# The last projection of a two-block model kernel: the fourth tile of tokens runs two steps behind the other three, activations are split two steps sooner, and the last pair's transposes move among the second half's products

## The reference

```
u = h @ w_in;  q, fz, i, gate = split(u, 4)          # 1024 -> 4 * 2048
o = hgrn2_chunk_scan(q, k, v, b)                     # 16 heads of 128
o = o * rsqrt(mean(o * o) + EPS) * norm_g            # per head
y = (o * silu(gate)) @ w_out                         # 2048 -> 1024: the last projection
h = h + y;  out = rms_norm(h, final_g)
```

## Time and profile before

| | us |
|---|---|
| median of 3 runs | 1507.29 |
| lowest, highest | 1507.28, 1510.85 |
| profiled execution, its own time | 1509.23 |
| span of the profile | 1507.5 |
| TensorE's mean granted clock | 0.99 of full |
| PE busy | 1454.2 (96%) |
| DVE busy | 871.4 (58%) |
| ACT busy | 563.1 (37%) |

### The profile page before, as it was taken

One profiled execution on the slowest core, in us unless ns is written; L12 is line 12 of the kernel. 1 busy time (PEld: TensorE's weight loads), 2 busy tenths in 40 slices (PEclk: granted clock), 3 DMA queues, 4 the chain that ended last, 5 costly groups with the idle time before them and its releaser, 6 DMA issues.

```text
span 1507.5 us, 18485 instructions
## 1 busy us (share of the span) xinstructions
PE 1454.2 (96%) x7204; PEld 1208.6 (80%) x7204; DVE 871.4 (58%) x1716; ACT 563.1 (37%) x1022; POOL 0.2 (0%) x4
## 2 busy tenths in 40 slices
PE   4999998999999999899999899999999999999897
PEld 4788887888888888888888787888888888888686
DVE  7877766443333335655547435325777878778435
ACT  6423345422232223533223234334444544445231
POOL 0000000000000000000000000000000000000000
PEclk9999999999999999999999999999999999999999
DMA  8646441353323333223233232332222222222121
GB/s 326 226 152 220 173 154 47 120 197 98 93 94 95 97 97 98 72 97 126 70 108 102 70 112 84 99 98 70 71 70 71 65 63 71 70 71 71 56 70 57
DMA packets 43719, 158.31 MB, mean 105 GB/s; under 512 B 4848, under 2 KB 5232, under 8 KB 43632
## 3 DMA queue, kind: packets, MB, share of 16 engines
q1 hardware_dynamic: 43632, 157.12, 31.9%
HBM read 155.00 MB, written 2.10 MB: 104 GB/s over the span
## 4 chain that ended last, share of the span: by engine, by line
PE 89%; DVE 6%; ACT 3%; issue 1%; DMA 1%; SPq 0%; ACTq 0%; DVEq 0%
PE PS L463 27%; PE PS L465 27%; PE PS L464 27%; PE PS L738 1%; PE PS L786 1%; PE PS L749 1%; PE PS L790 1%; PE PS L780 1%; DVE WL L915 1%; PE PS L758 1%; PE PS L766 1%; DVE RAW L885 1%; PE PS L814 1%; DMA X<-in_x 1%; DVE X L1030 1%
## 5 line engine op out<-in xcount | busy, mean ns | idle before, releaser
L463 PE MATMUL PS<-HH,WH 128*128 128x512 f32 (+1 forms) x1152 | 452.1, 392 | 4.4 <-ACT TMP L1688 2.3
L465 PE MATMUL PS<-HH,WL 128*128 128x512 f32 (+1 forms) x1152 | 437.3, 380 | 0.0
L464 PE MATMUL PS<-HL,WH 128*128 128x512 f32 (+1 forms) x1152 | 436.4, 379 | 0.0
L915 DVE TENSOR_TENSOR WL<-RAW,WH 128x1024 fp32r<-128x1024 f32 x225 | 273.6, 1219 | 83.7 <-ACT WH L1589 83.4
L1589 ACT ACTIVATE WH<-RAW 128x1024 fp32r<-128x1024 f32 x225 | 236.9, 1056 | 174.9 <-PE PS L465 134.6
L463 PEld LDWEIGHTS PS<-HH,WH 128*128 128x128 f32 x1152 | 218.2, 189 | 43.1 <-issue 3.7
L465 PEld LDWEIGHTS PS<-HH,WL 128*128 128x128 f32 x1152 | 217.9, 189 | 42.0
L464 PEld LDWEIGHTS PS<-HL,WH 128*128 128x128 f32 x1152 | 218.5, 190 | 37.0 <-issue 1.0
L463 PE MATMUL PS<-WH,ZH 128*128 128x512 f32 x400 | 157.0, 392 | 3.9 <-issue 3.9
L464 PE MATMUL PS<-WL,ZH 128*128 128x512 f32 x400 | 156.8, 392 | 0.0
L465 PE MATMUL PS<-WH,ZL 128*128 128x512 f32 x400 | 156.6, 391 | 0.0
(11 more groups left out here) (244 smaller groups left out, 1647.8 us busy)
## 6 DMA issues: line engine op xcount, KB each, us to landing
RAW<-in_w_fc SPq DMA_DIRECT2D x64, 512.0 KB, 3.5
RAW<-in_hgrn_in SPq DMA_DIRECT2D x64, 512.0 KB, 3.5
RAW<-in_ada SPq DMA_DIRECT2D x43, 512.0 KB, 4.7
RAW<-in_pool_in SPq DMA_DIRECT2D x40, 512.0 KB, 3.5
RAW<-in_w_in SPq DMA_DIRECT2D x27, 512.0 KB, 4.3
RAW<-in_pool_out SPq DMA_DIRECT2D x16, 512.0 KB, 3.5
RAW<-in_hgrn_out SPq DMA_DIRECT2D x16, 512.0 KB, 3.5
RAW<-in_w_out SPq DMA_DIRECT2D x8, 512.0 KB, 4.0
```

The source lines that it names most:

```text
L463: e.matmul(out, wh, xh, start=first, stop=False)
L464: e.matmul(out, wh, xl, start=False, stop=False)
L465: return e.matmul(out, wl, xh, start=False, stop=last)
L915: e.tensor_tensor(lo, raw(i), hi.bitcast(F32), ALU.subtract).then_inc(taken.sem, taken(i))
```

## The change

It keeps every product and every instruction's work; PE has 6256 rows of instructions before and after, and only their order differs.

1. `group` for the first half is replaced by `first_half`: 10 steps instead of 8. Step s issues k = s of tiles 0 to 2 (s < 8), then k = s - 2 of tile 3 (s > 1). A weight unit is released by tile 3's odd k, so two steps later. `mixing(15)` still starts after step 1.
2. ACT and DVE split k = 0 to 5 at n = 18 to 23 of head 15 (before: k = 0 to 3 at n = 20 to 23), and k = 6, 7 at steps 0 and 1 of the first half.
3. In the second half the transposes of heads 14 and 15 stand after k = 4 and k = 6 of tiles 0 to 2 (before: after k = 0 and k = 1). DVE and ACT take the weight units that used to stand behind them first.

```diff
--- before.py
+++ after.py
@@ -795,15 +795,6 @@
                     norms.append(two_norms(h - 1))
                 yield
 
-            def open_product(first, k, tiles):
-                hi, lo = (x[:, 512 * (k % 2):512 * (k % 2) + 512] for x in place(first + k // 2))
-                for t in tiles:
-                    b, cols = out_bank("hout", t, 1), slice(128 * t, 128 * t + 128)
-                    if k == 0:
-                        claim(b)
-                    m = three(PS[b][:, :], HH[:, k, cols], HL[:, k, cols], hi, lo, k == 0, False)
-                return m
-
             def two_norms(h):
 
                 for i in range(2):
@@ -816,12 +807,37 @@
                     m.then_inc(banks.full[RBK], banks.fill(("ho norm", h + i), RBK))
                     yield
 
+            def out_product(first, k, t, n):
+
+                hi, lo = (x[:, 512 * (k % 2):512 * (k % 2) + 512] for x in place(first + k // 2))
+                b, cols = out_bank("hout", t, n), slice(128 * t, 128 * t + 128)
+                if k == 0:
+                    claim(b)
+                return three(PS[b][:, :], HH[:, k, cols], HL[:, k, cols], hi, lo, k == 0, False)
+
+            def first_half():
+
+
+                first = p.unit
+                for step in range(10):
+                    if step < 8:
+                        if step % 2 == 0:
+                            next_unit()
+                        e.wait_ge(hlo.sem, hlo.of("hout", step))
+                        for t in range(3):
+                            out_product(first, step, t, 0)
+                    if step > 1:
+                        k = step - 2
+                        m = out_product(first, k, 3, 0)
+                        if k % 2:
+                            m.then_inc(read.sem, read("w", first + k // 2))
+                            wfree[first + k // 2] = read.sem, read.n
+                    yield
+
             norms = []
             turn, side = iter(()), iter(())
             for h in range(17):
-                steps = project(h) if h < 16 else group(
-                    None, [out_bank("hout", t, 0) for t in range(4)], True, "hout")
-                for n, _ in enumerate(steps):
+                for n, _ in enumerate(project(h) if h < 16 else first_half()):
                     if n in SIDE or h == 16:
                         next(side, None)
                         next(turn, None)
@@ -833,19 +849,21 @@
 
 
             turn = norms.pop()
+            next(turn)
             first = p.unit
-            for q in range(4):
-                next_unit()
-                for kk in range(2):
-                    open_product(first, 2 * q + kk, range(3))
+            for k in range(8):
+                if k % 2 == 0:
+                    next_unit()
+                for t in range(3):
+                    out_product(first, k, t, 1)
+                if k in (4, 6):
+                    next(turn)
                     next(turn, None)
-                    next(turn, None)
-            run(turn)
-            for q in range(4):
-                for kk in range(2):
-                    m = open_product(first, 2 * q + kk, (3,))
-                m.then_inc(read.sem, read("w", first + q))
-                wfree[first + q] = read.sem, read.n
+            for k in range(8):
+                m = out_product(first, k, 3, 1)
+                if k % 2:
+                    m.then_inc(read.sem, read("w", first + k // 2))
+                    wfree[first + k // 2] = read.sem, read.n
             rows("hout", 16, 8)
 
 
@@ -1529,11 +1547,10 @@
                 for n, _ in enumerate(project(h) if h < 16 else group()):
                     if n == (0 if h == 16 else 3) and gates:
                         gates.pop()()
-                    if h == 15 and n >= 20:
-                        split_z(n - 20)
-                    if h == 16 and n < 3:
-                        for k in ((4, 5), (6,), (7,))[n]:
-                            split_z(k)
+                    if h == 15 and n >= 18:
+                        split_z(n - 18)
+                    if h == 16 and n < 2:
+                        split_z(6 + n)
                     if n == 10 and prep:
                         ready_steps = prep.pop()
                     if n >= 10 or h:
@@ -1551,18 +1568,17 @@
 
 
             turn = norms.pop()
+            next(turn)
             first = p.unit
-            for q in range(4):
-                p.unit += 1
-                lo_to(min(p.unit + 2, first + 4))
-                for kk in range(2):
-                    next(turn, None)
-                    next(turn, None)
-            run(turn)
+            p.unit += 4
+            lo_to(first + 4)
             z_first(8)
-            lo_to(first + 6)
-            for q in range(4):
-                lo_to(first + 6 + q)
+            next(turn)
+            next(turn)
+            lo_to(first + 5)
+            next(turn)
+            for q in range(5):
+                lo_to(first + 5 + q)
             rows(16, 8)
             for t in range(4):
                 add("hout", t)
@@ -2049,17 +2064,13 @@
 
             turn = norms.pop()
             first = p.unit
-            for q in range(4):
-                p.unit += 1
-                hi_to(min(p.unit + 2, first + 4))
-                for kk in range(2):
-                    next(turn, None)
-                    next(turn, None)
+            p.unit += 4
+            hi_to(first + 3)
+            next(turn)
+            hi_to(first + 4)
             run(turn)
             z_first(8, gated)
-            hi_to(first + 6)
-            for q in range(4):
-                hi_to(first + 6 + q)
+            hi_to(first + 9)
             rows(16, gated, 8)
             for t in range(4):
                 e.wait_ge(*banks.taken(("hout", t, 0)))
```

## The result

| | before | changed |
|---|---|---|
| median of 8 runs | 1508.09 us | 1499.72 us |
| lowest to highest | 1505.87 to 1510.85 | 1497.67 to 1504.06 |
| profiled execution, its own time | 1509.23 | 1500.85 |
| span of the profile | 1507.5 | 1499.1 |

The ratio, taken from all runs and not from the medians, is 0.9947, with a 95% interval of 0.9936 to 0.9959. That is faster by more than the 0.3% that the prediction asked for: 8.0 us of 1508.09 (6.2 to 9.7); the medians differ by 8.4. The forecast was 8.7 us.

The account below looks back on a forecast made before the run. TensorE, busy 96% of the span, was taken as the bound, so only its waits and half clock could be regained: 10.3 less a new wait of 1.6 gives 8.7 us, so 1498.6 us from 1507.29; range 1496.5 to 1503.2.

Parts of the forecast that it names:

- the four waits of the earlier trace: TensorE's waits for L1376, L2016, the last projection's first product and L2005: 3.47, 2.42 and together 1.22 us, all to go.
- both stretches at half clock: TensorE at 1.2 GHz behind the waits for L1376 and L2016, costing 1.68 and 1.53 us, both to go.
- Splits sooner: DVE ahead of L1376: one more split (0.61) and the pair L1421, L1422 (0.67) make L1376 1.28 us later.
- Bank 2 comes free as TensorE arrives: Tile 3's first matmul: bank 2 free and TensorE there both at 1400.58; 0.0 us wait remains, up to 0.3.
- The new wait: TensorE at L749 waits 1.6 us for banks 3 and 4, whose copies stand behind L1376 and splits 6 and 7.
- Half clock behind it: Behind the wait at L749: forecast took 0; the rival had 1.7 us more, 1500.3 us, chance 0.12.
- The rival of the cause at 1433: Half clock behind the transposes was not the wait's, so its 1.53 us stays: 1500.1 us, chance 0.08.
- Late evacuations: ACT's evacuations a step late: once 1503.1 us, chance 0.05; at all three places 1512.1, chance 0.04; level 64 cover 1.2 us.

Follow-up runs that it names:

- the variant without any wait: Changed kernel, with DVE's release of bank 2 and copies out of banks 3 and 4 ahead of unit 2's remainder and splits 6 and 7; 1500.04 us, ratio 0.9947.
- only the splits sooner: Kernel before, with only the second part of the change, splits two steps sooner; first half and transposes as before; 1509.51 us, ratio 1.0014.
- the copies first: Changed kernel, with DVE's copies out of banks 3 and 4 ahead of splits 6 and 7; 1498.59 us, ratio 0.9934.
- a longer wait: Changed kernel, with the remainder of weight unit 3 also ahead of DVE's copies out of banks 3 and 4; 1502.27 us, ratio 0.9964.
- transposes as before: Kernel before, with parts one and two of the change (tile 3 and splits), transposes not moved; 1500.99 us, ratio 0.9955.
- only the transposes moved: Kernel before, with only the third part of the change; first half and splits as before; 1505.24 us, ratio 0.9973.
- splits where they were: Changed kernel, with ACT's and DVE's splits put back to their old steps; tile 3 delayed and transposes moved; 1503.38 us, ratio 0.9963.

## Why the prediction held

**The gain.** Forecast 8.7, measured 8.0 with 6.2 to 9.7. All of the four waits of the earlier trace rows went, as did both stretches at half clock. The two together were put at 10.3; the variant without any wait is 10.6 shorter than before in the stage. That the 8.38 between the two profiled executions lies so close to 8.7 is in part luck: the stage gave 7.15, and 1.22 came from the part ahead of it. The 10.3 also holds for one execution of the kernel before: 3.2 of it is half clock, and "only the splits sooner" had none behind the transposes, where 1.53 had been counted.

**Splits sooner.** That DVE's idle time would swallow split 0, that split 1 would start where split 0 had, and that L1376 would come 1.28 later: measured 1.27. The 0.6 that I expected of the splits alone was measured as 0.57, but by two errors that cancel, as shown there: their cost at bank 2 is 1.27.

**Bank 2 comes free as TensorE arrives.** Forecast: both at 1400.58, a wait of 0 to 0.3. The view marks no wait, but the starts show one of 0.20, in the changed kernel and with the copies first. The variant that frees bank 2 1.1 sooner gains 0.68 over the one with the copies first: 0.23 + 0.16 for the wait at L749, 0.20 for bank 2, and 0.09 that I can't place.

**The new wait.** Forecast 1.6, measured 1.42, and 1.58 with the 0.16 that a mark leaves out. The step's own number was the loss, so it was right to 0.02. Taking two splits away took 1.19 of it, adding a unit's remainder added 1.13.

**Half clock behind it.** I took none, with 0.12 for the rival. This is the term that was mis-sized in the profiled execution: it came, and cost 1.61. In the second profile of the same kernel and in the two variants with the same or a longer wait there (1.41 and 2.55) it did not. That explains the stage: 8.7 forecast, 7.15 with it, 8.76 without. How often it comes in the runs is open; two profiles of the changed kernel can't say it. That this half clock is the wait's doing is not shown either. The two variants with 0.23 us and no wait at L749 had none, but neither had three of the four profiles with a wait of 1.4 to 2.6 us there.

**The rival of the cause at 1433.** By that rival the half clock behind the transposes had another cause and would stay. It is gone in every kernel without that wait; but "only the splits sooner" and "transposes as before" kept a wait there (2.25 and 1.52) without half clock behind it. So in this stage it was never seen without such a wait, and such a wait does not always bring it. The rival is weakened by that, not refuted. The Trainium skill, "TensorE: Matmul & The Clock Gate", section "Why this matters for your kernels", asks for no idle gap of TensorE over about 3 us between bursts of matmuls. The traces do not bear that out as a limit: waits of 2.26 and 1.42 us had 0.51 behind them, and one of 3.21 us had full clock.

**Late evacuations.** The cover that I put at 1.2 us for level 64 was there: ACT's L2008 and L2013 run from 1415.41 to 1416.14, TensorE wants their banks at L780, 1417.27. The prediction did not name split 7. In the changed kernel ACT has done it by 1396.19, long before the copy of unit 4 at 1407.31; with the splits left in place it stood behind that copy and was the thing that failed, by 3.21 us.

## What to carry to other kernels

When a wait is removed by letting its consumer come later, look at what the same queue has to deliver next: here the copies out of banks 3 and 4 stood behind the late one, and cost 1.6 of 10.3 us. Work that two engines do in the order of a shared list of steps can often be put right by swapping two instructions on one of them; the swap of two splits gave 1.2 us in the stage for no work. And where runs spread by more than the effect, take the distance between two marks in the trace, one ahead of the change and one behind it, and look inside it too, since stretches at half clock come and go between executions: it came within 0.3 us of the expected sum in five of the eight runs, in one of them by two errors that cancel (the others missed by 1.9 us, for a stretch at half clock that did not come, by 0.7, of which 0.5 was a forgotten effect, and by 0.4), while the medians of five runs could not order the three best kernels.

## What the hardware showed beyond this

The same wait of TensorE goes with its lower clock level in one execution and not in another. The idle times over 1 us and what the trace shows at them, all in this stage:

| idle, us | kernel | clock at it |
|---|---|---|
| 5.35 | only the splits sooner | half, 1398.9 to 1405.7 |
| 3.31 | before | half, 3.4 us |
| 3.29 | only the transposes moved | half, 3.4 us, of which 0.4 before the wait ends |
| 3.21 | splits where they were | full |
| 2.55 | a longer wait | full |
| 2.26 | before | half, 3.5 us |
| 2.25 | only the splits sooner | full |
| 1.52 | transposes as before, at L805 | full |
| 1.42 | changed | half, 3.4 us |
| 1.43 | changed, once more | full |
| 1.41 | transposes as before, at L749 | full |

The windows of two of them, the first with 3.21 us of idle time and the second with 5.35:

```profile
1408.60:1412.00 3.40, 3.36 (x28) 2.76 (x28) 2.30 (x5) 0.53 (x2) 0.00 (x0) 1.00 0.02 5
```

```profile
1400.40:1405.60 5.20, 5.18 (x12) 4.12 (x13) 1.17 (x2) 0.00 (x0) 0.00 (x0) 0.50 0.32 101
```

The clock does not always fall at the end of the wait. With 5.35 us of idle time it fell 1.5 us before TensorE started again, and in the changed kernel 1.6 us after it, when TensorE was back at work (L749 starts at 1401.74; windows of 0.25 us give 1.00 up to 1403.25 and 0.64 and 0.50 after it). Length alone does not decide it: 1.42 had it and 3.21 had not. An estimate for the price of a wait of TensorE between 1.4 and 3.3 us is therefore the wait, and on top of it 1.5 to 1.7 us some of the time: in four of the ten waits of that length here.
